# Gate and final-norm rows: from diagonals and products with ones to a trip through DRAM

## What is computed

```python
# first block, for l in 0, 1
shift, scale, gate = split(silu(c) @ w_ada[l] + b_ada[l])      # three vectors of 2048
h = rmsnorm(x, norm_g[l]) * (1 + scale) + shift
z = h @ w_in[l]                                                # 2048 -> 13 pieces of 512
y = concat(four mixers of z) @ w_out[l]                        # 2048 -> 2048
x = x + gate * y
...
x = rmsnorm(x, final_g)
# second block, i = 0 (pool, also on ctx) and 1 (mla)
x = x + gate * rms_norm(y_lat, post_norm[i])
ctx = ctx + gate_c * rms_norm(y_ctx, post_norm[i])             # i = 0 alone
```

## Time and profile before

| | us |
|---|---|
| median of 3 runs | 2280.75 (2276.0 to 2283.2) |
| the profiled execution's own time | 2281.84 |
| its span, first to last instruction | 2280.2 |
| TensorE busy | 2193.2 (96% of the span) |
| VectorE busy | 1481.3 (65%) |
| ScalarE busy | 964.9 (42%) |
| mean granted TensorE clock | 0.986 |
| moved by DMA | 509.84 MB, 224 GB/s over the span |

### The profile page before, as it was taken

One profiled execution on the slowest core, in us unless ns is written; L12 is line 12 of the kernel. 1 busy time (PEld: TensorE's weight loads), 2 busy tenths in 40 slices (PEclk: granted clock), 3 DMA queues, 4 the chain that ended last, 5 costly groups with the idle time before them and its releaser, 6 DMA issues.

```text
span 2280.2 us, 33056 instructions
## 1 busy us (share of the span) xinstructions
PE 2193.2 (96%) x13686; PEld 1821.5 (80%) x13686; DVE 1481.3 (65%) x1904; ACT 964.9 (42%) x1337; POOL 200.9 (9%) x385
## 2 busy tenths in 40 slices
PE   5879999999899999999999999999999999999998
PEld 3668878887788877886788888888777989988876
DVE  0445778876646677764696757567966868544654
ACT  2324544454434644454642222223446534444443
POOL 2201110110011010100000101010100011000000
PEclk9989999999999999999999999999999999999999
DMA  9989787778599677668476646463875688422253
GB/s 359 401 263 310 260 289 238 250 259 290 153 283 336 212 270 240 215 222 296 161 260 198 190 134 216 134 213 121 288 249 191 219 262 277 144 75 64 79 189 134
DMA packets 225454, 509.84 MB, mean 224 GB/s; under 512 B 36064, under 2 KB 40288, under 8 KB 222752
## 3 DMA queue, kind: packets, MB, share of 16 engines
q1 hardware_dynamic: 170320, 300.49, 39.4%
q0 software_dynamic: 54304, 202.79, 26.2%
q10 hardware_dynamic: 688, 4.55, 0.5%
HBM read 499.38 MB, written 8.39 MB: 223 GB/s over the span
## 4 chain that ended last, share of the span: by engine, by line
PE 79%; DMA 9%; DVE 7%; ACT 2%; issue 2%; SPq 1%; POOL 0%; DVEq 0%; ACTq 0%; POOLq 0%
PE ps L767 22%; PE ps L768 21%; PE ps L769 21%; DMA w_raw<-in_w_in 5%; PE ps L823 3%; DVE ada_acc L2162 2%; DMA ada_raw<-in_ada_w 2%; PE ps L1434 1%; DVE wl L2242 1%; DMA w_raw<-in_w_out 1%; PE ps L895 1%; ACT wh L1538 1%; PE ps L951 1%; SPq L603 1%; PE ps L964 1%
## 5 line engine op out<-in xcount | busy, mean ns | idle before, releaser
L2249 DVE TENSOR_TENSOR wl<-w_raw,wh 128x1024 fp32r<-128x1024 f32 x280 | 335.5, 1223 | 259.6 <-ACT wh L1538 258.8
L1538 ACT ACTIVATE wh<-w_raw 128x1024 fp32r<-128x1024 f32 x280 | 291.7, 1055 | 381.0 <-PE ps L769 238.7
L1591 ACT ACTIVATE wh<-w_raw 128x1024 fp32r<-128x1024 f32 x220 | 230.7, 1058 | 433.6 <-PE ps L769 386.6
L767 PE MATMUL ps<-hh,wh 128*128 128x256 f32 x1280 | 372.8, 291 | 10.4 <-DVE hl L2302 7.5
L2242 DVE TENSOR_TENSOR wl<-w_raw,wh 128x1024 fp32r<-128x1024 f32 x220 | 266.9, 1222 | 178.3 <-ACT wh L1591 178.1
L768 PE MATMUL ps<-hh,wl 128*128 128x256 f32 x1280 | 360.8, 282 | 0.0
L769 PE MATMUL ps<-hl,wh 128*128 128x256 f32 x1280 | 360.3, 281 | 0.0
L2162 DVE SCALAR_TENSOR_TENSOR ada_acc<-ada_raw,cpad,ada_acc 128x1024 f32<-128x1024 f32 x262 | 328.5, 1281 | 15.9 <-DMA ada_raw<-in_ada_w 13.9
L767 PEld LDWEIGHTS ps<-hh,wh 128*128 128x128 f32 x1280 | 242.5, 189 | 38.3 <-issue 24.3
L767 PE MATMUL ps<-wh,act_hl 128*128 128x512 f32 x640 | 256.6, 401 | 0.2 <-DVE wl L2242 0.2
L768 PE MATMUL ps<-wh,act_hl 128*128 128x512 f32 x640 | 253.3, 396 | 0.0
(11 more groups left out here) (374 smaller groups left out, 3396.7 us busy)
## 6 DMA issues: line engine op xcount, KB each, us to landing
ada_raw<-in_ada_w POOLq DMA_DIRECT2D x272, 512.0 KB, 5.1
w_raw<-in_w_in SPq DMA_DIRECT2D x208, 512.0 KB, 5.8
w_raw<-in_pool_in SPq DMA_DIRECT2D x72, 512.0 KB, 4.6
w_raw<-in_w_out SPq DMA_DIRECT2D x64, 512.0 KB, 5.5
w_raw<-in_mla_in SPq DMA_DIRECT2D x56, 512.0 KB, 4.8
ada_fourth<-in_ada_w POOLq DMA_DIRECT2D x48, 512.0 KB, 6.3
w_raw<-in_pool_out SPq DMA_DIRECT2D x48, 512.0 KB, 5.1
w_raw<-in_mla_out SPq DMA_DIRECT2D x32, 512.0 KB, 4.1
```

Of the source, the lines that this page charges most:

```text
L767: pe.matmul(dst, ah, bh, start=start, stop=False, skip_group_check=True)
L1538: act.activation(wh[:, g % RING, :], w_raw[:, g % RING, :], ACT.Copy).then_inc(w_hi, 1)
L1591: act.activation(wh[:, r, :], w_raw[:, r, :], ACT.Copy).then_inc(w_hi, 1)
L2249: dve.tensor_tensor(wl[:, g % RING, :], w_raw[:, g % RING, :], wh[:, g % RING, :].bitcast(F32), ALU.subtract).then_inc(w_lo, 1)
```

## The change

A small tensor `rows_d` of six rows x 2048 in DRAM is added. A vector is written to it by a transfer from its column form (`as_rows`: each fp32 value goes to an address of its own, 128 partitions x 16 columns), and comes back by a transfer that reads 512 of its values 128 times, once for each partition (`wide_row`). All of these are issued on ScalarE's queue. The diagonals, the products with ones and the copies out of PSUM go, in all four places. `gate_norm(1)` moves ahead, to the fourth gate piece of the attention layer.

- `final_g` is written at step 10 of layer 0, and its four quarters are read back in layer 1 at steps 27, 30, 32 and 34.
- A layer's gate is written in two halves, at steps 25 and 30 (8 columns each). Quarters 0 and 1 are read at step 27 into `dec` and `ptr`, quarters 2 and 3 at steps 31 and 33.
- Both gates of the pooling layer are written where `gate_diagonals` stood, 16 columns each, and read by eight transfers three converted slots later.
- The attention layer's gate is written before the first pair of heads and read as one transfer of 2048 columns between the pairs.

```diff
+    rows_d = nc.dram_tensor("rows_d", (6, D), F32, kind="Internal").ap()
+        gate_rows = (dec[:, :], ptr[:, 0, :])
+        def as_rows(r, n, c0=0, c1=KT):
+            a = rows_d[r:r + n, c0 * P:c1 * P].rearrange("v (c p) -> p v c", p=P)
+            return a if n > 1 else a[:, 0, :]
+        def wide_row(r, q, n=1):
+            return bass.AP(rows_d.tensor, r * D + q * GRP, [[0, P], [1, n * GRP]])
...
-                def row_of(n):
-                    pe.wait_ge(dg_ok, n + 1)
-                    if n > 4 * l:
-                        pe.wait_ge(row_ok, n)
-                    pe.matmul(ps[:, 7, :], ones[:, :], diag, start=True, stop=True).then_inc(row_ps, 1)
...
-                            gate_row(0, 0, 6)
-                            gate_row(0, 1, 7)
-                            gate_row(1, 0, 4)
-                            gate_row(1, 1, 5)
...
-                    for j in range(4):
-                        mm = pe.matmul(ps[:, j, :], ones[:, :], dgm[:, j * 512:(j + 1) * 512], start=True, stop=True)
...
+                    if l == 0 and t == CONV0:
+                        act.dma_start(as_rows(0, 1), cl("final_g", 0, KT), allow_slow_non_contiguous=True).then_inc(t_dg, 16)
+                    if t == SMALL_STEP - 1:
+                        act.wait_ge(ada_read, ada_event(l, GATE_AT[l]) + 1)
+                        act.dma_start(as_rows(1 + l, 1, 0, 8), mod[:, 0, 32:40], allow_slow_non_contiguous=True).then_inc(dg_ok, 16)
+                    if t == OUT_STEP:
+                        act.wait_ge(dg_ok, 32 * l + 16)
+                        act.wait_ge(rt_p, l * HEADS + HEADS)
+                        act.dma_start(gate_rows[0], wide_row(1 + l, 0)).then_inc(row_ok, 16)
+                        act.wait_ge(na_pv, l * HEADS + HEADS)
+                        act.dma_start(gate_rows[1], wide_row(1 + l, 1)).then_inc(row_ps, 16)
+                        if l:
+                            act.wait_ge(t_dg, 16)
+                    if t == OUT_STEP + 3:
+                        act.wait_ge(ada_read, ada_event(l, OUT_STEP + 1) + 1)
+                        act.dma_start(as_rows(1 + l, 1, 8), mod[:, 0, 40:48], allow_slow_non_contiguous=True).then_inc(dg_ok, 16)
+                    if t in (OUT_STEP + 4, OUT_STEP + 6):
                         q = (t - OUT_STEP) // 2
-                        n = l * 4 + (2 * q if l else q)
-                        act.wait_ge(row_ps, n + 1)
-                        if q:
-                            act.wait_ge(res_ok, l * 4 + q)
-                        act.activation(row, ps[:, 7, :], ACT.Copy).then_inc(row_ok, 1)
...
+                        act.wait_ge(dg_ok, 32 * l + 32)
+                        act.wait_ge(gated, l * 4 + q - 1)
+                        act.dma_start(gate_rows[q % 2], wide_row(1 + l, q)).then_inc(row_ps if q % 2 else row_ok, 16)
+                    if l and t in (OUT_STEP, OUT_STEP + 3, OUT_STEP + 5, OUT_STEP + 7):
                         q = (t - OUT_STEP) // 2
-                        act.wait_ge(row_ps, 4 + 2 * q + 2)
                         if q:
                             act.wait_ge(xg_ok, q)
-                        act.activation(frow, ps[:, 7, :], ACT.Copy).then_inc(row_ok, 1)
+                        act.dma_start(frow, wide_row(0, q)).then_inc(t_ps, 16)
...
-            def gate_diagonals():
+            def gates_to_rows():
                 act.wait_ge(t_gp, 1)
+                for v in range(2):
+                    act.dma_start(as_rows(3 + v, 1), mod[:, v, 32:48], allow_slow_non_contiguous=True).then_inc(t_dg, 16)
+
+            def gate_rows_in():
+                act.wait_ge(t_dg, 48)
                 act.wait_ge(p_olo, 8)
-                act.wait_ge(tabs_in, 32)
                 for v in range(2):
                     for q in range(4):
-                        for j in range(4):
-                            ins = act.activation(dg2(v, q)[:, j * P:(j + 1) * P], idm, ACT.Copy,
-                                                 scale=mod[:, v, 32 + 4 * q + j:33 + 4 * q + j])
-                ins.then_inc(t_dg, 1)
+                        act.dma_start(gate2(v, q), wide_row(3 + v, q)).then_inc(t_ps, 16)
...
+                    if kind == "out" and i == 1 and s == 6:
+                        gate_rows_in()
...
+            act.wait_ge(t_gp, 2)
+            act.dma_start(as_rows(5, 1), mod[:, 0, 32:48], allow_slow_non_contiguous=True).then_inc(t_dg, 16)
...
+            act.dma_start(rowm, wide_row(5, 0, 4)).then_inc(t_row, 16)
...
-                        act.activation(rowm, bank(0, 4), ACT.Copy).then_inc(t_row, 1)
...
-                for j in range(4):
-                    ins = dve.tensor_scalar(diag[:, j * P:(j + 1) * P], ident, src[:, j:j + 1], None, ALU.mult)
-                ins.then_inc(dg_ok, 1)
...
-                dve.tensor_copy(x4[:, 2 * v + 1, a], ps[:, row_, :]).then_inc(t_row, 1)
-                dve.wait_ge(t_row, rows - 4)
...
-                            ins = dve.tensor_scalar(dgm[:, j * P:(j + 1) * P], idm, mod[:, 0, 32 + j:33 + j], None,
-                                                    ALU.mult)
```

85 lines of the change are left out of this document (28 added, 57 removed).

## The result

The change makes the kernel slower: 2304.79 us (2296.19 to 2307.18) against 2279.54 us (2276.0 to 2283.2) before, a ratio of 1.0105 (95% interval 1.0086 to 1.0125). Measured again beside the experiments it was 1.0072 (1.0048 to 1.0096). So it costs 16 to 24 us where 12.5 us of gain were forecast, and the time lies outside the range. The profiled execution took 2306.35 us, its span is 2304.3.

A forecast was written before the change was run, and what follows sets the result against it. TensorE was taken as the bound, busy 2193.2 of 2280.2 us. 17.2 + 1.8 - 1.3 - 1.5 - 0.5 - 0.2 - 3.0 = 12.5 us gained, so median 2280.75 to about 2268; range 2258 to 2283.

The forecast's parts named there:

- The element writes: Issuing single values on ScalarE's queue: 0.2 us for layers' half gates, 3 us (0 to 14) for the pooling layer's gates.
- 13.2 us of cover: Pooling layer: ScalarE was already busy before `krf` is needed, so being held that long by the issues costs nothing.
- The second rival: Element writes are slow, c per value and DMA engine, holding ScalarE in the pooling layer; at 0.25 us, 2291 us; chance 0.14.
- breakeven in c: Second rival: the 15.5 us gain is used up when 156c = 28.7, at c = 0.18 us.
- The rule against the change: Skill's advice against strided last dimensions and transfers under 512 B; unpriced, taken to support the upper half of the bound.
- Products with ones: 24 removed TensorE rows at 0.86 us each; four lie ahead of existing waits, so 20 rows give 17.2 us.
- the ceiling of 20.6: Gain if all 24 removed rows of products with ones were collected.
- VectorE late in the pooling layer: Context's quarter 2: TensorE comes 5.2 us earlier against a VectorE lead of 3.8, so 1.3 us (0 to 2.1) are lost.
- Bytes in layer 1: Reads of three rows, 0.79 MB, ahead of full DMA engines at 1025 to 1050: 1.5 us lost (0 to 2.0).
- chain 1.3: Layer 1, 1050 to 1065: scaled identities and a copy leave VectorE's and ScalarE's chain, gaining 1.3 us of the term's 1.8.
- Waits: Steps 27 and 31 hidden, the latter barely; `gate_rows_in` some 14 us after issue, within the 3 us; attention layer nothing.
- The signs to look for: TensorE busy down some 20 us, idle times at 1065 and 1734 changed, lengths of the pooling layer's two write issues.

The follow-up runs named there:

- turned: Changed kernel, but VectorE turns gate columns into rows by four 32x32 transposes per gate, written as 512 B runs: 2268.66 us against 2283.82 before, ratio 0.9934.
- writes_alone: Kernel before, nothing removed, plus the change's eight element writes on ScalarE's queue, which nobody reads or waits for: 2303.54 us against 2283.82, ratio 1.010.
- probes: Kernel before, with small transfers behind its last output, one at a time, each beside four 512 KB loads; loads took 5.3 to 12.6 us by form.
- turned_once: As `turned`, but one 128x32 transpose per set of gate columns and four transfers of 128 B runs per write: 2264.04 us against 2280.67 before, ratio 0.9931.
- runs: Changed kernel, but each partition's 8 or 16 values are neighbours in DRAM, so 128 runs of 32 or 64 B: 2262.49 us against 2283.82 before, ratio 0.9915.
- no_wait: Changed kernel with its element writes, but rows read from input x and no waits for the writes: 2300.01 us against 2280.67 before, ratio 1.009.

## Why the prediction was wrong, point by point

- **The element writes: the step that failed.** The prediction asked how long ScalarE is held by issuing them and when they land, and priced that at 3.0 us. ScalarE was held 0.38 and 2.53 us, well inside the 13.2 us of cover. Their cost is on other queues: loads of 512 KB that take 20.8 us instead of 4.5. The price of all element writes together is 31 to 39 us (change against `turned`), not 3.2; added to the kernel before, as in `writes_alone`, they cost 19.7. No row of before could show it, because nothing there wrote single values; the bounds of 0 to 14 us were made from the 256 B runs of the earlier trace rows and only for the queue that issues. A bound on what the writes do to the other queues was missing.
- **The second rival** had the right sign and the wrong mechanism. It let ScalarE's queue drain slowly, from a price c for each value, and held against itself that the load stops when ScalarE stops. The packets of single values themselves took some 10 ns; the number of values hardly matters (128 as bad as 1024 in the probes); and the loads under way stay slow until the write has landed, whatever ScalarE does. Its breakeven in c has no meaning.
- **The rule against the change** was cited. The Trainium skill (DMA: Bandwidth & Descriptors, Rules for kernel authors) says that a strided last dimension becomes one descriptor for each element, and advises against it; the trace agrees (1040 packets for a write of 1024 values). Its Specifications put the limit at 512 B. Here the loads beside 1024 runs of 64 B or 1024 values 64 B apart took 5.8 to 5.9 us against 5.2 to 5.5 beside runs of 128 or 512 B, and beside 128 touching values 12.3. So shortness alone is cheap, and the neighbourhood is what costs; I had let the rule speak only for the upper half of a bound that was made for the wrong thing. The Trainium skill also (VectorE: DVE Perf Modes, The three transpose paths) puts a plain strided copy used as a transpose at 19 times the time of the DMA's own transpose where the innermost destination stride is large. No run here has that other transpose, so nothing here bears on the comparison. Among the probes' strided writes the large stride was the quick one: at 512 B 5.4 us, at 4 B 12.4.
- **Products with ones: right.** In `turned` the lateness falls by 0.46 and 0.41 us over the two slots behind a row of layer 0 (0.87; I had 0.86), by 3.4 and 1.7 us at the two places of the context's quarter 2 (six rows, 5.1; I had 5.2) and by 3.5 in the attention layer (four rows; 3.4). 17.2 + 1.8 - 1.3 - 1.5 - 0.5 - 0.2 = 15.5 was the sum without elements; `turned` gained 15.1 by the ratio, `turned_once` 15.7, `runs` 19.4. That `turned` meets the sum so closely is partly luck: it has transposes on VectorE, which the sum did not have, and loses 3.3 us in the pooling layer where `runs` loses nothing. The kernel that differs from the change by the addresses alone is `runs`, and for it the sum is 4 us too small; it nearly reached the ceiling of 20.6.
- **VectorE late in the pooling layer: right.** Behind the context's quarter 2 I forecast 1.3 us lost again at the slot that begins at 1703.34. It is 1.5 us in the changed kernel and in `runs`, 1.0 in `turned`, and 0.4 at the slot ahead in all three.
- **Bytes in layer 1.** Around the reads of three rows `turned` loses 1.9 and 1.6 us at two slots, where TensorE waits for adaptation weights, more than my 1.5. The idle time before 1065.01 (4.39 us), which I let grow, is 4.61 us in `turned` and 1.34 in `runs`, where TensorE had waited 0.68 and 4.12 us for adaptation weights earlier in the stretch. From slot 252 to 264 the difference only goes from -2.9 to -2.2 in `turned`, and from -6.8 to -8.4 in `runs`. The forecast for this stretch, chain 1.3 against bytes 1.5, is between them.
- **Waits.** Step 27: the write landed 10.3 and 10.6 us after issue, forecast more than 20 us of room; hidden. Step 31: I had 11.1 + 2 us to land; it was 20.2 in layer 0 and 11.1 in layer 1, so in layer 0 ScalarE issued the next read at 566.77, the moment it landed. That would look like the cause, but `no_wait` takes the wait away and the 2.9 us of TensorE's idle time at the same slot stay. `gate_rows_in` came 33.6 us after the issue, not 14. The attention layer was right: nothing.
- **The signs to look for** that the prediction named fit the failure badly: it said a second issue under 10 us would mean "I am right or too careful". It was 2.53 us, and TensorE did sit idle before the adaptation result's turn, which was meant to go with a long issue. TensorE's busy time was to fall by some 20 us: it fell by 8.3 in the changed kernel and by 21.1 in `runs`. The idle time at the slot of 1065 was to be 5 to 8 us and was 1.35, after TensorE had waited 7.83 and 1.59 us for adaptation weights earlier; the one at 1734 was to be about 1.5 and is 1.55 in `turned` and `runs`. The transfers' rate in the stretches, which shows it at once, was not among the signs.

## What to carry to other kernels

Don't spread a column vector over DRAM value by value while loads run: here 128 touching writes of 4 B were enough to slow the transfers of other queues for some 10 us. Turn it on the chip first (a transpose costs 0.2 us on VectorE), write runs of 32 B or more, and the trip through DRAM gives what it promises, here 15 us or 0.7%. When a change adds a transfer of a new kind, price what it does to the other queues' transfers, not only its own issue, bytes and landing, and look in the profile for engines that are busy and move little.

## What the runs showed of the hardware that I had not expected

- Touching 4 B writes stall the loads beside them, whether 128 or 1024 of them (12.3 and 12.6 us to land instead of 5.3), and spacing them by 32 B or more takes nearly all of it away (5.8 to 6.0).
- The stall outlives the packets and ends with the write's landing: all 1024 values of a half gate went out within 1.6 us of 491.2, the write landed at 500.2, and the loads stayed at 34 to 67 GB/s until 501; in the attention layer a load 4 us behind the last value moved 33 GB/s, and 157 GB/s were moved from 2022 on, with the landing at 2022.6.
- In such a stretch the DMA share reads 0.8 to 1.3 with 43 to 114 GB/s moved: a tenth of the packets of 2 KB and more is recorded as over 1.7 us long between 494 and 501 us, against 0.2 us between 480 and 490, so the share alone looks like a full load.
- TensorE's granted clock went to 0.50 while it stood in the pooling layer, and its first products ran at 0.50 from 1655 to 1660.
